# Two value projections and the second output matrix as seven quarter products, and expert loads placed between dense units

## What is computed

```python
h = rms_norm_2(x, norm_mix)                      # 256 x 1024
hq, hf, hi, hog, dq, dk, dv, gate_hg, gate_da = split(h @ w_in)
o_hg = hgrn2_chunked(hq, 1 - f, hi, log f)       # hi: the values
o_hg = rms_norm_2(o_hg, g) * silu(hog);  y_hg = o_hg @ w_branch_hg
o_da = diff_attention(rope(norm(dq)), rope(norm(dk)), dv, lam)
y_da = rms_norm_2(o_da, g2) @ w_branch_da
mixed = sigmoid(gate_hg) * y_hg + sigmoid(gate_da) * y_da
x = x + mixed @ w_out                            # 1024 x 1024
x = x + hier_moe(rms_norm_2(x, norm_moe), ...)   # top 2 of 32 experts
```

## Time and profile before

| | |
|---|---|
| median of three runs | 1079.41 us |
| the profiled execution, its own time | 1080.32 us |
| span in the profile | 1078.4 us |
| TensorE matmul busy | 936.4 us, 87% |
| TensorE weight load busy | 552.0 us, 51% |
| VectorE busy | 444.9 us, 41% |
| ScalarE busy | 255.6 us, 24% |
| read from HBM | 291.18 MB |

### The profile page before, as it was taken

The page is one execution under the profiler, slowest core; times in us unless marked ns, Lnnn a source line. Parts: engine busy times, 40 slices in busy tenths (PEclk is TensorE's granted clock), DMA queues, the critical chain, the costliest instruction groups (busy, mean ns, idle before and its releaser), DMA issues.

```text
span 1078.4 us, 12700 instructions
## 1 busy us (share of the span) xinstructions
PE 936.4 (87%) x5074; PEld 552.0 (51%) x5074; DVE 444.9 (41%) x740; ACT 255.6 (24%) x626; POOL 155.9 (14%) x107
## 2 busy tenths in 40 slices
PE   8999999999999999999999998957756667675856
PEld 6665655668888857545788753423311213131312
DVE  6879899835722445682634213211101102020201
ACT  4585977414421012412312020000000000000000
POOL 0886677820000000000000000000000000000000
PEclk9999999999999999999999999998878978798888
DMA  9444243252246453353224799999999999999997
GB/s 364 190 156 156 79 156 130 105 196 90 79 183 285 156 181 144 129 196 125 84 104 156 305 427 382 429 424 427 425 428 427 428 426 430 428 428 428 427 428 320
DMA packets 29121, 292.91 MB, mean 272 GB/s; under 512 B 7568, under 2 KB 8592, under 8 KB 10640
## 3 DMA queue, kind: packets, MB, share of 16 engines
q1 hardware_dynamic: 28928, 292.24, 66.7%
q10 hardware_dynamic: 144, 0.00, 0.0%
HBM read 291.18 MB, written 1.05 MB: 271 GB/s over the span
## 4 chain that ended last, share of the span: by engine, by line
PE 53%; DMA 34%; DVE 6%; ACT 2%; issue 2%; POOL 2%; SPq 0%; DVEq 0%; POOLq 0%; ACTq 0%
DMA mem<-in_experts 32%; PE psum L342 16%; PE psum L333 7%; PE psum L349 7%; PE psum L321 4%; PE psum L1641 3%; PE psum L326 3%; PE psum L2015 2%; PE psum L972 2%; PE psum L1990 1%; PE psum L1668 1%; DVE mem L2200 1%; PE psum L1658 1%; PE psum L855 1%; DMA mem<-in_front 1%
## 5 line engine op out<-in xcount | busy, mean ns | idle before, releaser
L1641 PE MATMUL psum<-mem 128*32 128x512 f32 x1016 | 150.3, 725 | 80.5 <-DMA mem<-in_experts 80.5
L333 PE MATMUL psum<-mem,hT 128*128 128x512 f32 x288 | 127.8, 600 | 0.5 <-issue 0.5
L1641 PEld LDWEIGHTS psum<-mem 128*32 128x32 f32 x1016 | 31.6, 122 | 180.7 <-DMA mem<-in_experts 113.4
L342 PE MATMUL psum<-hT,mem 128*128 128x256 f32 x512 | 115.2, 381 | 0.0
L342 PEld LDWEIGHTS psum<-hT,mem 128*128 128x128 f32 x512 | 95.6, 190 | 15.9 <-issue 2.9
L333 PEld LDWEIGHTS psum<-mem,hT 128*128 128x128 f32 x288 | 56.3, 199 | 65.4 <-issue 65.4
L1801 DVE SCALAR_TENSOR_TENSOR mem<-mem,psum 128x512 f32<-128x512 f32 x8 | 5.5, 687 | 159.0 <-ACT mem L1543 159.0
L342 PE MATMUL psum<-mem 128*128 128x256 f32 x320 | 69.7, 379 | 0.0
L342 PEld LDWEIGHTS psum<-mem 128*128 128x128 f32 x320 | 60.6, 190 | 8.1
L349 PE MATMUL psum<-hT,mem 128*128 128x256 f32 x256 | 57.6, 382 | 0.0
L1668 PE MATMUL psum<-mem 128*32 128x512 f32 x244 | 39.4, 756 | 20.5 <-DMA mem<-in_experts 16.2
(11 more groups left out here) (387 smaller groups left out, 1325.5 us busy)
## 6 DMA issues: line engine op xcount, KB each, us to landing
mem<-in_experts SPq DMA_DIRECT2D x87, 2048.0 KB, 35.6
mem<-in_front SPq DMA_DIRECT2D x37, 2048.0 KB, 7.8
mem<-in_experts SPq DMA_DIRECT2D x15, 1024.0 KB, 33.8
mem<-in_wo_units SPq DMA_DIRECT2D x2, 2048.0 KB, 14.5
con<-in_constants SPq DMA_DIRECT2D x1, 1035.0 KB, 18.7
xn<-in_xT SPq DMA_DIRECT2D x2, 512.0 KB, 5.6
mem<-in_front SPq DMA_DIRECT2D x2, 512.0 KB, 7.5
mem<-in_front SPq DMA_DIRECT2D x1, 1024.0 KB, 10.3
```

The costliest lines, as they stand in the source:

```text
L333: ins = pe.matmul(dst, tokens[:, k, i], w[:, k, :], start=(k == 0), stop=(k == KD - 1))
L342: ins = pe.matmul(dst[:, at:at + T], w[:, k, P * m:P * m + P], rhs[:, k, :], start=(k == 0), stop=(k == nk - 1))
L1641: ins = pe.matmul(banks[m // 2 % 2][32 * q:32 * q + 32, :], xgT[:, k, 32 * q:32 * q + 32], w[q][:, FF * kk:FF * kk + FF], start=(k == 0), ...
```

## The change

1. `hi` and `dv` become seven quarter products (28 matmuls of 128x512 in place of 32), with four new sums of 128x2048 on VectorE and five combining reads; ScalarE copies out products 0 and 2. `dv` is not computed after the turning of k but with `hi`; q is turned after hog. `rope2` is split, and the reads of the new products are put between its parts.
2. The second product of `dq`, `dk` waits for two sums of weights, no longer for four.
3. `w_out` becomes seven quarter products, with four sums of weights, four of activations, and nine additions onto x in place of four. The first two sums of weights stand among the reads of `bda`. `w_sum2` is kept in `hT`.
4. Loads: slot 4 in two halves (after `gda0` and after `bda`), slots 6, 7 and a quarter of unit 9 after `gda1`, the rest after `wout1`; `eleventh` waits only for the turning of the attention's output. The work areas of unit 10 and of the router's small tiles are shifted by 56 floats so that this fits.
5. Fills and loads are renumbered, and the turning of x and the logits follow the order in which quarters of x become ready.

The diff's core:

```diff
@@ sync
             for n in range(n_units1 + SLOTS_BLOCKS, n_blocks):
+                if FRONT[n][0] == "dv":
+                    sp.wait_ge(quarter_sums.sem, SUMS_DQK)
                 load_unit(sp, n)
+                if FRONT[n][0] == "gda0":
+                    tp.to_read(sp, TP_DQ + 1)
+                    load_ahead(sp, 4, slice(0, 2048))
+                elif FRONT[n][0] == "gda1":
+                    tp.to_read(sp, TP_HG + 1)
+                    load_ahead(sp, 6)
+                    load_ahead(sp, 7)
+                    load_tenth(sp, 0)
+                elif FRONT[n][0] == "bda":
+                    sp.wait_ge(ds_full, 8)
+                    load_ahead(sp, 4, slice(2048, 4096))
+                elif FRONT[n][0] == "wout1":
+                    sp.wait_ge(da_full, 8)
+                    load_ahead(sp, 5)
+                    sp.wait_ge(ods_ready, 1)
+                    for q in (2, 3):
+                        load_tenth(sp, q)
+            for s in range(2):
+                tp.to_read(sp, TP_DO + s)
+            sp.dma_start(eleventh, A["experts"][0, UNITS - 2]).then_inc(eleventh_loaded, 16)
+            for name in ("bda", "wout1", "wout0"):
+                pj.to_read(sp, last_fill[name])
+                load_ahead(sp, order[name] % SLOTS_BLOCKS)
+                if name == "wout1":
                     load_sixth(sp, 1)
@@ scalar
             head_sqrt(0)
+            evacuate(hv_first, PJ_HI)
             head_sqrt(1)
+            evacuate(hi_tok[:, 0, :], PJ_HI + 2)
             evacuate_turned(dT_[1], TP_DK, 2)
             for i in range(2):
                 pj.to_read(act, PJ_HOG + i)
                 act.activation(og[:, i, :], pj.tile(PJ_HOG + i)[:, :], ACT.Tanh, scale=0.5).then_inc(th_hog, 1)
+            evacuate_turned(dT_[0], TP_DQ, 2)
@@ tensor
-            pe.wait_ge(quarter_sums.sem, SUMS_DQK)
+            pe.wait_ge(quarter_sums.sem, SUMS_DQK2)
             quarter_product(PJ_DQ + 1, x_sum2, dqk_sum2, True)
...
+            quarter_product(PJ_HI, hT[:, 0:4, 0:P], b11, True)
+            pe.wait_ge(quarter_sums.sem, SUMS_HV2)
+            quarter_product(PJ_HI + 1, x_sum2, hv_sum2, True)
+            quarter_product(PJ_HI + 2, hT[:, 4:8, 0:P], b21, False)
+            pe.wait_ge(quarter_sums.sem, SUMS_HV1)
+            quarter_product(PJ_HI + 3, x_diff1, b11, False)
...
+            pe.wait_ge(quarter_sums.sem, SUMS_HV)
+            quarter_product(PJ_HI + 6, hT[:, 4:8, P:T], b21, False)
...
+            pe.wait_ge(m2_done, 4)
+            pe.wait_ge(quarter_sums.sem, SUMS_M2)
+            quarter_product(PJ_WOUT + 1, m_sum2_, w_sum2, True)
+            quarter_product(PJ_WOUT + 2, m2T[:, 4:8, 0:P], b21, False)
+            pe.wait_ge(quarter_sums.sem, SUMS_W1)
+            quarter_product(PJ_WOUT + 3, m_diff1_, b11, False)
+            quarter_product(PJ_WOUT + 4, m_diff3_, b12, True)
+            turn_x(0)
+            quarter_product(PJ_WOUT + 5, m_diff4_, b22, False)
+            turn_x(1)
+            pe.wait_ge(quarter_sums.sem, SUMS_W4)
+            quarter_product(PJ_WOUT + 6, m2T[:, 4:8, P:T], b21, False)
...
+            turn_x(2)
+            logits(0, True)
+            logits(1, True)
+            turn_x(3)
+            logits(2, False).then_inc(logits_full, 1)
+            logits(3, False).then_inc(logits_full, 1)
@@ vector
             take_product(4, k_high, k_high, even, ALU.subtract)
+            hv11, hv21, hv12, hv22 = quarters(dve, "hi", "dv")
+            link(dve, dve.tensor_tensor(hv12, hv12, hv22, ALU.add), quarter_sums)
             take_product(5, k_low, odd, first_, ALU.subtract)
+            link(dve, dve.tensor_tensor(hv_sum2, hv11, hv12, ALU.add), quarter_sums)
+            take_product(6, q_high, q_high, even, ALU.add)
             norm_sums2(1)
...
             norm_sums2(0)
+            take_hv(1, hi_tok[:, 1, :], hv_first, hv_odd, ALU.subtract)
+            link(dve, dve.tensor_tensor(hv11, hv_sum2, hv22, ALU.subtract), quarter_sums)
+            pj.to_read(dve, PJ_HI + 2)
+            link(dve, dve.tensor_tensor(hv21, hv_sum2, hv21, ALU.add), quarter_sums)
+            scale2(1)
+            take_hv(3, dv_tok[:, 1, :], hv_odd, hv_first, ALU.subtract)
+            rope2(1, 0)
...
+                if n == 1:
+                    dve.wait_ge(m2_done, 2)
+                    form(m_diff3_, a11, a21, ALU.subtract, SUMS_M3)
+                    b11, b21, b12, b22 = quarters(dve, "wout0", "wout1")
+                    form(b12, b12, b22, ALU.add, SUMS_W3)
+                elif n == 2:
+                    form(w_sum2, b11, b12, ALU.add, SUMS_W2)
+            form(m_sum2_, m_diff3_, a22, ALU.add, SUMS_M2)
...
+            add_product(0, x12, -0.5, last=False)
+            add_product(0, x22, -0.5, last=False)
+            add_product(0, x21, 0.5)
+            form(b11, w_sum2, b22, ALU.subtract, SUMS_W1)
+            add_product(1, x21, -0.5)
+            add_product(2, x11, 0.5)
+            form(b21, w_sum2, b21, ALU.add, SUMS_W4)
...
```

More of the change, by code:

```diff
@@ L384, in load_expert_unit, with load_ahead @@
                 sp.dma_start(ring[:, s, :], src).then_inc(slot_loaded[s], 16)
-        def load_ahead(sp, slot):
+        def load_ahead(sp, slot, c=slice(0, UNIT)):
             u = {there: unit for unit, there in IN_RING.items()}[slot]
-            sp.dma_start(ring[:, slot, :], A["experts"][0, u]).then_inc(slot_loaded[slot], 16)
+            sp.dma_start(ring[:, slot, c], A["experts"][0, u, :, c]).then_inc(slot_loaded[slot], 16)
         def load_tenth(sp, q):
@@ L1336, in build @@
         (PJ_HF, PJ_HQ, PJ_DQ, PJ_DK, PJ_HI, PJ_DV, PJ_HOG, PJ_O, PJ_DA, PJ_BHG, PJ_BDA, PJ_WOUT, PJ_END2) = (
-            int(n) for n in PJ_END1 + np.cumsum([0, 4, 4, 7, 0, 2, 2, 2, 2, 8, 4, 4, 4]))
+            int(n) for n in PJ_END1 + np.cumsum([0, 4, 4, 7, 0, 7, 0, 2, 2, 8, 4, 4, 7]))
         def gate_fill(n):
@@ L1352, in da_outputs @@
             return tp.tile(da_turned(a))[:, 384:512]
-        for name, s in ([("hf", PJ_HF + 3), ("hq", PJ_HQ + 3), ("dq", PJ_DQ + 3), ("dk", PJ_DQ + 5), ("hi", PJ_HI + 1),
-                         ("dv", PJ_DV + 1), ("hog", PJ_HOG + 1), ("bhg", PJ_BHG + 3), ("bda", PJ_BDA + 3)]
+        for name, s in ([("hf", PJ_HF + 3), ("hq", PJ_HQ + 3), ("dq", PJ_DQ + 2), ("dk", PJ_DQ + 5), ("hi", PJ_HI + 6),
+                         ("dv", PJ_HI + 5), ("hog", PJ_HOG + 1), ("bhg", PJ_BHG + 3), ("bda", PJ_BDA + 3)]
                         + [(f"ghg{n}", gate_fill(2 * n + 1)) for n in range(2)]
                         + [(f"gda{n}", gate_fill(2 * n + 5)) for n in range(2)]
-                        + [(f"wout{n}", PJ_WOUT + 2 * n + 1) for n in range(2)]):
+                        + [("wout0", PJ_WOUT + 6), ("wout1", PJ_WOUT + 5)]):
             last_fill[name] = s
@@ L1949, in _ @@
             evacuate_turned(daT_, TP_DO, 2)
-            for n in range(4):
-                i, c = n % 2, n // 2
-                pj.after_read(act, PJ_WOUT + n)
+            for n, last in enumerate((2, 4, 5, 6)):
+                i, c = QUARTERS_OF_X[n]
+                pj.after_read(act, PJ_WOUT + last)
                 if n >= 2:
@@ L1958, in _ @@
                 if n == 1:
-                    for i in range(2):
-                        turned_x(act, TP_R + i)
+                    act.wait_ge(quarter_sums.sem, SUMS_W4)
+                    for m in range(2):
+                        turned_x(act, TP_R + m)
                 if n == 2:
```

141 lines of the change are left out of this document (71 added, 70 removed).

## The result

| | before | after |
|---|---|---|
| median, us | 1079.74 (1079.29 to 1080.51, 4 runs) | 1073.14 (1071.65 to 1074.07, 4 runs) |
| profiled execution, us | 1080.32, span 1078.4 | 1072.93, span 1071.0 |

The ratio of the times is 0.994, with a 95% interval of 0.9927 to 0.9954: 6.6 us faster. The forecast was 1072.7 with a range of 1071.0 to 1075.4, so it was right, and 0.4 us low.

What follows compares the result with a forecast made beforehand. TensorE was taken to bound the kernel up to the experts' first matmuls and DMA after, the end being the first used unit plus 423.4 us. 3.64 + 3.1 = 6.7 us earlier gave a median of 1072.7, range 1071.0 to 1075.4.

Steps and rivals of the forecast that it cites:

- Step 1: Second product of dq, dk: begins without waiting for the fourth sum, so hi begins 0.55 us earlier.
- Step 2: hi and dv: four fewer matmuls save 3.43 us; VectorE keeps up, no stall, with 0 and 0.5 as bounds.
- Step 3: q's transposes after hog: copies end 0.36 us later against TensorE, L2045 begins near 505.05, 3.64 us earlier so far.
- Step 4: w_out: four fewer matmuls save 3.43 us, less a 0.3 stall and 0.1 restart, plus 0.1 at the logits; net -3.1.
- Step 5: Expert loads: moves cost nothing and lift a limit; without them the queue ends 2 us past the first use.
- half-gain case: Hi/dv and w_out stages: VectorE's additions become TensorE's wait, costing 2.8 us, time 1075.5; 11%.
- slower case: w_out: loads issued behind `wout1` share its queue rate, second product 12.3 us late, time 1085.0; 4%.
- first rival: Start of the expert stream: DMA, not TensorE, sets the hand-over, so gain 0 and time stays 1079.4; 4%.

Runs made afterwards that it cites:

- hv_only: Changed kernel with w_out projected as before; hi and dv by quarters and the moved loads stay: 1076.04 us, ratio 0.9971.
- wout_only: Changed kernel with hi, dv and the wait for all four sums as before; w_out by quarters and moved loads stay: 1076.07 us, ratio 0.9971.
- loads_only: Kernel before with only the expert loads in their new places, all products as before: 1078.35 us, ratio 0.9998.
- one_sum_twice: Changed kernel with VectorE forming hv_sum2 a second time (2.3 us) ahead of the sum for product 3 of hi, dv: 1075.91 us, ratio 0.9969.
- loads_late: Changed kernel with the first group's expert loads back behind wout1, in the old order: 1072.42 us, ratio 0.9936.
- load_before_wout1: Changed kernel with one 2 MB expert load (slot 5) issued just ahead of wout1 instead of just behind it: 1078.55 us, ratio 0.9992.
- smoother: Changed kernel with q turned in the middle of hog and two scan differences moved behind VectorE's first read: 1072.81 us, ratio 0.9936.
- smoother_beside: The code of smoother run again, against the changed kernel: 1073.47 us, ratio 0.995.
- loads_late_beside: The code of loads_late run again beside the changed kernel on one chip: 1072.67 us, ratio 0.9941.

## Why the prediction was right, step by step

**What bounds it: right.** The end is the first used unit plus a fixed stretch: 423.4 was said, and 422.6 to 423.0 is measured wherever the tail ran at full clock. A saving on TensorE ahead of the hand-over comes through whole as far as the medians can tell, in each part alone (`hv_only`, `wout_only`) and in both. A saving on the queue alone is worth nothing (`loads_only`).

**Step 1 (-0.55): right.** From the first product of dq and dk to the first one of hi and dv it is 25.15 before (464.40 - 439.25) and 24.65 after (463.57 - 438.92), 0.50 less. The 0.35 of idleness at 449.74 that is left hangs on the read of product 0's bank (L2249), as the step said.

**Step 2 (-3.43, no stall): right.** The 28 matmuls run without a bracket. The walk through VectorE had the third sum done at 474.0 for a TensorE that wants it at 474.1. It was done at 473.73 and wanted at 473.88: a slack of 0.15 where 0.1 was forecast. `one_sum_twice` shows that this row was the right one to look at. The four products of 5.00 us ended at 501.0, forecast at 501.

**Step 3 (-3.64 at the state's first matmuls): nearly right.** It is 504.97 against 508.69, and less the 0.33 of the first layer 3.39. The missing 0.25 is mostly the ScalarE chain: from hog's last matmul to these it was 1.16 us before, and is now 2.56 with 0.87 of q's transposes in it, so 0.53 later where 0.36 was said. The new order has TensorE wait in two places for the copies, not in one. Another 0.05 is missing from step 1.

**Step 4 (-3.1): nearly right.** From w_out's first product to the last logits it is 32.68 us before (612.98 to 645.66) and 29.73 after (609.26 to 638.99): 2.95 less. The stall ahead of the second product was forecast at 0.3 with 0.1 for the restart. The second product begins 3.68 us behind the first (609.10 to 612.78), where 3.43 is the length of one, and the third 3.51 behind the second: 0.33 together, 0.07 less than forecast. The logits, which were to gain 0.1, lost 0.15: 1.71 + 1.88 us for the 16 matmuls against 0.82 + 2.62. These two terms make 2.95 of the 3.1.

**Step 5 (the loads cost nothing): right; (they lift a limit): worth almost nothing.** The queue was said to be 2 us late without them, and by the estimate above it was, by 1.9. Of this at most 0.4 us reached the end, so the moves are worth less than a measurement can tell. The step that failed is the one that took this lateness for a limit on the end, as the expectation for `loads_late` then did with 1.0 to 1.6 us. I had added up the bytes, and had not asked what a queue that runs dry loses when it starts again: 1.6 us in its first 10.

**Sum, right.** 0.33 from the first layer, 6.35 for the 6.7 of steps 1 to 4, and 0.7 from the tail, which the range had as 1 us either way, make the 7.39 of the two profiled executions. The first and the last are the luck of these executions. Over the medians it is 6.6 (1079.74 to 1073.14), 0.1 less than the sum said, and the rest of the 0.4 us is the reference, which stood at 1079.41 when I forecast. Only the middle term is the change. The places that the prediction named in time (L2045 near 505.0, w_out near 609.2, the first L384 near 648.2) were met within 0.1 us, and 0.33 of that is the first layer too.

**The rivals.** The half-gain case would have shown TensorE idle by over 0.5 us ahead of a quarter product; the longest wait is 0.35. The slower case needed `wout1` to land over 12 us after its issue; it landed 8.8 after. Where `load_before_wout1` did make it 12.8, and `wout1` landed 4.9 us later than in the changed kernel, 5.3 us of the gain were gone by the traces and 5.7 by the medians. The first rival stood on the trace's DMA at 1.00 for 413 us, and `loads_only` against `hv_only` and `wout_only` settles it. The Trainium skill (Perfetto Trace Analysis, "Identifying the Most-Contended Engine") says to optimize the most contended engine first, with HBM utilization as the measure for DMA, and for TensorE the share of its peak work and the busy share of the weight loads, not of the matmuls. The prediction took DMA from one stretch and gave it to the whole kernel. Over the whole span the page of the kernel before has 66.7% for the queue, 51% for weight loads and 87% for matmuls, so which engine the rule names depends on the measure. The runs refute the step from the rule to a sum of 0: time taken off TensorE was not lost, and loads moved earlier alone gave nothing. What fewer bytes in the stream would give, no run here shows. The section after it ("Optimization Strategy") says that the most contended engine can change over time, and by the two stretches above that is the case here.

## What to carry to other kernels

Where a kernel hands over from a stretch that one engine bounds to a stream that another bounds, and the stream can't start before the first engine has used something, read the end as that moment plus a constant: what is saved before it comes through whole, in whatever part it is made. When matmuls are traded for additions on another engine, follow the one result that is wanted soonest after it can be begun. Its slack was 0.15 us in a stretch where that engine idled for 7, and a further addition of 2.3 us there took 2.5 us of the gain back by the traces, 3.0 by the medians. And where a queue runs dry before such a stream, count what it loses in starting again before moving loads ahead of it: here that was as much as the lateness that the moves took away.

## What the runs showed of the hardware

- **The granted clock fell behind the logits in some executions and not in others.** It was down to 0.50 in 4 of the 14 that were profiled: in both of `smoother` and `smoother_beside`, which are the same code, at two different points, and in `loads_only` and `load_before_wout1`. In `smoother` 8 matmuls took 3.24 us instead of 2.05. There TensorE had been busy for 2.41 of the 4 us before, and for the same 2.41 in `loads_late_beside`, where the clock stayed. In the other three it had been busy without a break. In the tail the end came 422.6 to 423.0 us behind the hand-over where the clock was 1.00 (2.4 GHz) from 1060 to 1064, and 423.3 to 424.6 where it was 0.50 to 0.59 there, so at 1.2 GHz for most of the time.
- **In the batches looked at, the queue kept the order of its issues, at a small price for the first.** A unit of 2.097 MB landed 7.7 to 8.0 us after its issue with nothing issued right behind it (dense units of the changed kernel from 449 to 580). It landed after 8.5 to 8.9 as `wout1`, or the load in front of it, with others behind within 0.8 us. The one behind landed at 12.8 to 13.4, about one unit's time later. The first load of the second group took 7.6 to 8.8 on a queue that was empty or nearly so.
- **A queue that had run dry lost about 1.6 us when it started again.** In the 10 us behind the first issue it moved 356 GB/s in the changed kernel, against 426 in `loads_late`, where it never stood still.
